# A hybrid decoder layer on eight cores: first tile taken by feature quarters, half of the own activations built during the attention heads, memory copies split over two engines, four output buffers

## What is computed

```python
h = rmsnorm(x, g_pre)
u, v, z_a, c_q, c_kv, k_rope, z_b, q_m, z_m = split(h @ w_in)
y_a = chunked_spatial_gating(u, v, ...) * silu(z_a)      # masked 128x128 per group
y_b = latent_attention(c_q, c_kv, k_rope, ...) * silu(z_b)  # 16 heads, causal
y_m = memory_attention(q_m, mem, ...) * silu(z_m)        # 4 heads into 256 memory tokens
p = einsum('bsnc,ncd->bsnd', stack(y_a, y_b, y_m), w_branch)
merged = sum(sigmoid(h @ w_gate + b_gate) * p, axis=branches)
out = x + rmsnorm(merged @ w_out, g_post)
```

## Time and profile before

| | |
|---|---|
| median of 3 runs | 3443.63 us (3431.74 to 3857.7) |
| the profiled execution | 3429.86 us; its span, first to last instruction of the slowest core, 3428.0 us |
| spans of the cores | 3419.5 to 3428.0 us; mean granted clock 0.981 or 0.982 on all |
| busy | PE 3213.7 us (94%), DVE 1064.1 (31%), ACT 1006.6 (29%), POOL 152.8 (4%) |
| DMA | 208 MB moved; 369.85 MB read from HBM |
| load of one tile, issue to landing | median 16.2 us |
| PE's rate over the tiles | the query latents (line 512) start at 249.05, 293.10 and 336.81 us: 44 us for two tiles |
| the chain that ended last | PE 87%, DVE 5%, DMA 3%, issue 2%, ACT 2% |

### The profile page before, as it was taken

How to read it: one execution, slowest core, us unless ns; L and a number is a source line. 1 busy time by engine, 2 the same in 40 slices (tenths; PEclk the granted TensorE clock), 3 DMA queues, 4 the chain that set the end, 5 groups by cost and what they waited for, 6 DMA issues and landing times.

```text
span 3428.0 us, 62567 instructions; the slowest of 8 cores (3419.5 to 3428.0 us)
## 1 busy us (share of the span) xinstructions
PE 3213.7 (94%) x26432; PEld 1983.9 (58%) x26432; DVE 1064.1 (31%) x1691; ACT 1006.6 (29%) x1192; POOL 152.8 (4%) x289
## 2 busy tenths in 40 slices
PE   2799979999999999999998999889999999999997
PEld 1455557777777777777775544444444444444443
DVE  3444453333333333333334000542524111111115
ACT  1455534444444444444443111011111000000011
POOL 1000000000000000000000111000000000000000
PEclk9899999999999999999999999999999999999998
DMA  8455400000000000000204867344543544445465
GB/s 122 75 99 94 81 4 8 8 8 8 8 8 8 8 8 8 8 8 8 32 14 124 141 111 127 66 80 74 96 80 66 79 75 77 77 74 80 74 135 172
DMA packets 51683, 208.14 MB, mean 61 GB/s; under 512 B 5712, under 2 KB 9936, under 8 KB 47184
## 3 DMA queue, kind: packets, MB, share of 16 engines
q0 software_dynamic: 44496, 174.15, 31.3%
q1 hardware_dynamic: 6912, 29.99, 2.9%
HBM read 369.85 MB, written 8.39 MB: 110 GB/s over the span
## 4 chain that ended last, share of the span: by engine, by line
PE 87%; DVE 5%; DMA 3%; issue 2%; ACT 2%; DVEq 0%; POOL 0%; SPq 0%; ACTq 0%; POOLq 0%
PE ps L312 23%; PE ps L1270 10%; PE ps L790 8%; PE ps L755 7%; PE ps L763 7%; PE ps L731 6%; PE ps L711 6%; PE ps L514 4%; PE ps L1147 3%; PE ps L1317 2%; PE ps L1075 2%; PE ps L758 2%; PE ps L682 1%; PE ps L1052 1%; DMA y<-AR 1%
## 5 line engine op out<-in xcount | busy, mean ns | idle before, releaser
L775 ACT ACTIVATE AR<-ps 128x768 bf16<-128x768 f32 (+1 forms) x656 | 603.6, 920 | 759.5 <-PE ps L763 755.0
L312 PE MATMUL ps<-AR 128*128 128x512 bf16 x3584 | 790.0, 380 | 10.5 <-DVE AR L875 10.5
L312 PEld LDWEIGHTS ps<-AR 128*128 128x128 bf16 x3584 | 350.9, 98 | 430.5 <-issue 14.3
L755 PE MATMUL ps<-AR 128*128 128x256 bf16 (+2 forms) x2176 | 400.5, 279 | 1.1 <-DVE AR L697 1.1
L790 PE MATMUL ps<-AR 128*128 128x129 bf16 x4608 | 372.7, 220 | 1.6 <-ACT AR L775 1.6
L763 PE MATMUL ps<-AR 128*128 128x256 bf16 (+2 forms) x2176 | 358.4, 279 | 0.0
L514 PE MATMUL ps<-AR 128*128 128x512 bf16 x1024 | 274.0, 397 | 76.4 <-DVE AR L422 76.4
L790 PEld LDWEIGHTS ps<-AR 128*128 128x128 bf16 x4608 | 303.2, 98 | 70.3 <-issue 3.3
L1270 PE MATMUL ps<-AR 128*128 128x512 bf16 x1536 | 341.2, 380 | 0.0
L715 DVE CAST AR<-ps 128x512 bf16<-128x512 f32 x256 | 176.9, 691 | 386.5 <-PE ps L711 385.0
L731 PE MATMUL ps<-AR 128*128 128x128 bf16 x4096 | 290.1, 220 | 4.8 <-DVE AR L556 3.7
(11 more groups left out here) (155 smaller groups left out, 2307.9 us busy)
## 6 DMA issues: line engine op xcount, KB each, us to landing
AR<-wts POOLq DMA_DIRECT2D x256, 512.0 KB, 5.8
AR<-xaT POOLq DMA_DIRECT2D x15, 2048.0 KB, 16.2
AR<-xoT SPq DMA_DIRECT2D x16, 512.0 KB, 16.2
AR<-xo SPq DMA_DIRECT2D x8, 1024.0 KB, 8.5
y<-AR SPq DMA_DIRECT2D x8, 1024.0 KB, 11.1
AR<-rows SPq DMA_DIRECT2D x12, 256.0 KB, 6.5
AR<-wcA POOLq DMA_DIRECT2D x4, 576.0 KB, 17.6
AR<-xaT POOLq DMA_DIRECT2D x4, 512.0 KB, 20.1
```

What stands on the lines that cost most here:

```text
L312: ins = h.matmul(ps[:, out_pair_b + half, :], w3[:, k, :], act3[:, k, half * 512:(half + 1) * 512], start=(k == 0), stop=(k == 15))
L755: h.matmul(ps[:, sb + r, i * n:(i + 1) * n], kT[:, kb * 128:(kb + 1) * 128], q_[:, c0:c1], start=(i == 0), stop=False, skip_group_check=True)
L775: sc.add("act", lambda h: h.activation(out=pT[pt][:, :, 0:w], in_=ps[:, sb:sb + 2, 0:w], func=AF.Exp), reads=pregs(sb), writes=(("pT", pt),))
```

## The change

Five edits.

- **Start.** `wcA` and `wcQ` get pages of their own (80 to 97 and 98 to 113 KB), each quarter of `wcA` too. The second tile's load, now in four parts, and then `wcQ` are issued right behind the first tile. The first tile runs by feature quarters: quarter q of all four blocks, then q + 1. DVE scales quarter q one operation of the angles later than before; cosine and sine stand behind the first tile's copies on ACT. The second tile makes its query latent behind its last block instead of its first. The head weights' first load moves from behind tile 0 to behind tile 2.
- **Own activations.** `rstd_o` is inverted in eight pieces in steps 4 to 11 of the first head. Slices 0 to 7 of `hT` lie at 165 to 180 KB and are built in heads 1 to 8, one each: its load at step 0, its scaling at step 26, through two buffers at 137 and 141 KB. Slices 8 to 15 (0 to 15 KB) are loaded and scaled in the last head. The weight ring is 181, 185 and 16 to 28 KB; two pieces of it instead of four are fetched ahead of the last head. The first `proj` waits for `hT` in three parts.
- **Memory attention.** Every second copy of `Ah` goes to ACT. The reciprocal of 1024 columns is cut into four of 256, each with one piece of the next head behind it.
- **Output.** Four buffers each for x and for the result; product and sum by half rows, each half stored as soon as it is done; four loads of x ahead instead of two.
- Addresses of `wo` and `junk` follow.

```diff
-    wc = v3(80, 16, 1088)
+    wca = v3(80, 16, 576)
+    wcq = v3(98, 16, 512)
...
+    load_xa(1, 4)
+    sc.dma("pool", lambda h, sem: h.dma_start(out=wcq[:, :, :], in_=wcQ_d[:, :, :]).then_inc(sem, 16), "wcQ", 1, writes=("wcQ",))
...
+        if u == 0:
+            banks = [rot("mb", 4) for _ in range(4)]
+            for q in range(4):
+                for b in range(4):
+                    lat(b, banks[b], q, 0)
+            for b in range(4):
+                lat_out(b, banks[b])
+            for op in tops[-2:]:
+                op()
+        else:
+            for b in range(4):
...
+                accs = [(b, 0)] + ([(4, 1)] if own and b == (3 if u == 1 else 0) else [])
...
-    sc.add("dve", lambda h: h.reciprocal(out=rstd_o, in_=rstd_o), reads=("rstd_o",), writes=("rstd_o",))
...
+    HT_KB = [165 + 2 * k for k in range(8)] + [2 * k for k in range(8)]
+    STG_KB = [32 + 4 * i for i in range(8)] + [137, 141]
...
-    RING = (165, 169, 173, 177, 181, 185)
+    RING = (181, 185, 16, 20, 24, 28)
...
             if i == n_ab:
+                for k in range(8, 16):
+                    load_stg(k)
+                wsz.prefetch()
                 sc.dma("pool", lambda h, sem: h.dma_start(out=v2(189, 4096), in_=memT[:, :]).then_inc(sem, 16), "memn", 1, writes=("memn",))
-                wsz.prefetch()
-                for k in range(8):
-                    load_stg(k)
-            if i > n_ab and i - n_ab - 1 < 8:
-                scale_stg(i - n_ab - 1)
-                load_stg(i - n_ab + 7)
+            if i >= n_ab + 5 and i - n_ab - 5 < 8:
+                scale_stg(8 + i - n_ab - 5)
+        if hd == 0 and i >= 4 and i < 12:
+            sl = slice((i - 4) * 128, (i - 3) * 128)
+            sc.add("dve", lambda h, sl=sl: h.reciprocal(out=rstd_o[:, sl], in_=rstd_o[:, sl]), reads=("rstd_o",), writes=("rstd_o",))
+        if 1 <= hd < 9:
+            if i == 0:
+                load_stg(hd - 1)
+            if i == n_ab:
+                scale_stg(hd - 1)
...
-    for k in range(8, 16):
-        scale_stg(k)
...
+                if q % 2:
+                    sc.add("act", lambda h: h.activation(out=dst, in_=ps[:, bank, :], func=AF.Copy, scale=MSC), reads=pregs(bank, 1), writes=(("Ah", hm % 2, q),))
...
-        sc.add("dve", lambda h, b=b: h.reciprocal(out=rs, in_=pair(b)), reads=pregs(b), writes=("rs",))
-        for un in nxt[4:8]:
-            un()
+        for q in range(4):
+            sl = slice(q * 256, q * 256 + 256)
+            sc.add("dve", lambda h, b=b, sl=sl: h.reciprocal(out=rs[:, sl], in_=pair(b)[:, sl]), reads=pregs(b), writes=("rs",))
+            for un in nxt[4 + q:5 + q]:
+                un()
...
+        for hf in range(2):
+            hs = slice(hf * 1024, hf * 1024 + 1024)
+            src = obuf[:, j, :] if hf == 0 else pair(b)
...
+            sc.dma("sp", lambda h, sem, j=j, pj=pj, hs=hs: h.dma_start(out=y_d[j * 128:(j + 1) * 128, hs], in_=yo[pj][:, hs]).then_inc(sem, 16),
+                   "yout%d%d" % (pj, hf), 1, reads=(("yo", pj, hf),))
```

More of the change, by code:

```diff
@@ L306, in pregs, with mm32 @@
         return tuple("ps%d" % (b + i) for i in range(n))
-    def mm32(out_pair_b, w3, act3, h):
+    def mm32(out_pair_b, w3, act3, h, ks):
         ins = None
-        for k in range(16):
+        for k in ks:
             for half in range(2):
-                ins = h.matmul(ps[:, out_pair_b + half, :], w3[:, k, :], act3[:, k, half * 512:(half + 1) * 512],
+                ins = h.matmul(ps[:, out_pair_b + half, :], w3[:, k, :], act3(k)[:, half * 512:(half + 1) * 512],
                                start=(k == 0), stop=(k == 15))
@@ L364, in build @@
         place(("kpe2", n), 64 + n, 1)
-    wc = v3(80, 16, 1088)
+    wca = v3(80, 16, 576)
+    wcq = v3(98, 16, 512)
     for q in range(4):
-        sc.place(("wcA", q), *[(80 * 1024 + k * 2176, 1152) for k in range(4 * q, 4 * q + 4)])
-    sc.place("wcQ", *[(80 * 1024 + k * 2176 + 1152, 1024) for k in range(16)])
+        place(("wcA", q), 80 + 4.5 * q, 4.5)
+    place("wcQ", 98, 16)
     xa = [v3(114 + 16 * i, 16, 512) for i in range(2)]
@@ L468, in build @@
                      [("cos", tabs[:, :, 0, :], v16, slice(0, P), KPE), ("sin", tabs[:, :, 1, :], v16, slice(0, P), KPE)])
-    for i, op in enumerate(tops):
+    for i, op in enumerate(tops[:-2]):
         op()
-        if i in (3, 5, 7, 9):
-            q = (i - 3) // 2
-            scale_w(range(4 * q, 4 * q + 4), 0, 576, ("wcA", q))
+        if i in (4, 6, 8, 10):
+            q = (i - 4) // 2
+            scale_w(range(4 * q, 4 * q + 4), wca, ("wcA", q))
     def ang_own(add, a, ra):
@@ L521, in tile_main, with lat, mm @@
-            if b == 1 and u > 0:
-                tile_tail(u - 1)
+            if u > 0:
+                break
+        def lat(b, bank, q, is_q):
+            def mm(h):
+                ins = None
+                for k in range(4 * q, 4 * q + 4):
+                    xs = xt[:, k, b * 128:(b + 1) * 128]
+                    if is_q:
+                        ins = h.matmul(ps[:, bank, :], xs, wcq[:, k, :], start=(k == 0), stop=(k == 15))
+                    else:
+                        h.matmul(ps[:, bank, :], xs, wca[:, k, 0:512], start=(k == 0), stop=(k == 15))
+                        ins = h.matmul(ps[:, kr, b * 64:(b + 1) * 64], xs, wca[:, k, 512:576],
+                                       start=(k == 0 and (u > 0 or b == 0)), stop=(k == 15), skip_group_check=(u == 0))
+                return ins
+            sc.add("pe", mm, reads=(("xa", xb_, q), "wcQ" if is_q else ("wcA", q)), writes=pregs(bank, 1) + (() if is_q else pregs(kr, 1)))
@@ L970, in proj @@
         b = next_pair()
-        sc.add("pe", lambda h: mm32(b, w3, act3, h), reads=(wr,) + tuple(act_regs), writes=pregs(b))
+        for ks in parts:
+            sc.add("pe", lambda h, ks=ks: mm32(b, w3, act3, h, ks), reads=(wr,) + tuple(act_regs[ks.start:ks.stop]), writes=pregs(b))
         return b
@@ L1300, in build @@
     place("gpb", 113, 8)
-    for i in range(2):
-        place(("xob", i), 121 + 8 * i, 8)
-        place(("yo", i), 137 + 52 * i, 8)
-    place("junk", 197, 2)
+    for i in range(NY):
+        place(("xob", i), XO_KB[i], 8)
+        for hf in range(2):
+            place(("yo", i, hf), YO_KB[i] + 4 * hf, 4)
+    place("junk", 161, 2)
     sc.dma("sp", lambda h, sem: h.dma_start(out=gpb, in_=rows_d[0:1, ROW_GPOST:ROW_GPOST + 2048].to_broadcast([P, 2048])).then_inc(sem, 16),
@@ L1322, in build @@
     oss = stat[:, 0:32]
-    load_xob(0)
-    load_xob(1)
+    for j in range(NY):
+        load_xob(j)
     for grp in range(2):
@@ L1363, in build @@
         sems[s] = es.enter_context(nc.semaphore("s%d" % i))
-    final = [("dma:yout0", 64), ("dma:yout1", 64)]
+    final = [("dma:yout%d%d" % (i, hf), 16 * (8 // NY)) for i in range(NY) for hf in range(2)]
     with nc.Block() as block:
```

119 lines of the change are left out of this document (58 added, 61 removed).

## The result

The changed kernel takes 3353.75 us (median; lowest 3342.81), the kernel before 3431.74 us beside it on the same chip: a ratio of 0.9741, 95% interval 0.9707 to 0.9775, so 2.6% faster. Predicted were 3345 us and a range of 3332 to 3370. Two of the five executions of the changed kernel had one or both dies at a much lower clock and took 3880.39 and 3887.55 us; the ratio leaves them out, as it does the one of 3857.7 us of the kernel before.

A forecast was written before the change was run, and what follows sets the result against it. PE was taken as full (87% of the span), gaining only at its few waits and behind its last matmul. Gains 47 + 15.5 + 0.5 + 13 + 11 = 87 from 3429.9 gave 3343, stated as 3345 us, range 3332 to 3370.

The forecast's parts named there:

- Start: First tiles: own pages and earlier loads let the third tile start at 83.4 us instead of 130.3, gain 47.
- Own activations: End of last head: fewer late slices, closing not held up, first projection at the upper clock, gain 15.5 us.
- Heads: Eight heads: one more DVE scaling each costs PE 0 (0 to +9) us; `rstd_o` inverse in pieces gives −0.5.
- Memory: Memory attention: quartered reciprocal removes most of PE's 5.61 us wait; 4.7 us in three heads, −0.3 in the last, gain 13.
- the new wait of 2 us: Memory attention: next scores wait for the second product's copy, 2 us in place of the removed 5.6.
- Output: Output stage: with four buffers DVE needs 5.9 us per block, under PE's 6.9, and follows PE; gain 11 us.
- Shared landing: Start: second tile and `wcQ` share the engines with earlier loads, all landing near 62; 19 us lost, 3364; chance 0.10.
- DVE holding up POOL's transfers: Start: DVE's work on the angles keeps POOL from writing descriptors, `wcQ` 25 us later, 3370; chance 0.04.
- Quicker transfers: Start: longer rows load at 210 GB/s, second tile and `wcQ` down at 54, 8 us sooner, 3337; chance 0.05.

The follow-up runs named there:

- two-buffer kernel: Changed kernel with two output buffers each for results and inputs instead of four, half-row stores kept: output's first matmul to the end 123.2 us, profiled execution 3387.17 us.
- four scalings a head: Changed kernel with each of the eight scalings of own x in heads 1 to 8 done four times: profiled execution 3393.95 us.
- four more edits: Changed kernel plus second tile reordered around `wcQ`, memset of the ones column alone, whole reciprocal, all copies of pieces 4 to 7 by ACT: ratio to before 0.9733.

## Why the prediction was right, and where it was not

**Start (−47, measured −47.5).** Each step came: first matmul at 14, `wcQ` at 61.2, the sums at 79.1, third tile at 82.8. The text was right that the first tile, and with it the order by quarters, "is not what sets the second and third tile". What it didn't say is which edit carries the gain: with the own pages taken away 44.7 us are lost, with the quarters none.

**Own activations (−15.5, measured −17.3).** The number holds, its cause only in part. The prediction gave it to the eight slices moved into the heads and to a slice that lands before the closing. The slices moved are worth 4.0 (7 in the mean over the cores). The step it left out is the division of the first projection, 7.1 us (5 in the mean). With all slices at the end it covers most of DVE's scalings, and the slices moved shorten what it has to cover: two covers over one wait. What the division is worth when the slices are moved was not run.

**Heads (0, and −0.5 for the inverse of `rstd_o`).** PE's waits for the first query copies are 14.2 us, 14.6 before. Right, with a cover of 0.3 us. Ahead of the first head it is −1.1.

**Memory (−13, measured −10.4).** The mechanism was right, the sizes were off by a little each. A quarter of the reciprocal takes 1.76 + 0.1, not 1.69, so four take 7.34 (2194.30 in the last head) and not 6.8, and the periods are 30.2 and not 29.9. The prediction took 34.6 for all three periods of before, by one row; they were 34.62, 34.37 and 34.26. It gave the new wait of 2 us no cost in clock: on core 5 the clock fell behind all three of these waits, and where that reached into the scores (64 matmuls in 14.4 us instead of 13.97) the period was 30.6. The last head, from its scores to the next stage, takes 27.85 us and not 26.6, 1.3 more instead of 0.3. In the two-buffer kernel, whose memory stage is the same and whose scores all kept the upper clock, the stretch was −11.5.

**Output (−11, measured −12.0).** Right in size for core 5, which is where its rows were read; on the other cores, which stores had held up less, the gain is 5 to 10 us. "With four buffers" was not the only way to it: two buffers with half-row stores give nearly all of it too.

**Rivals.** Shared landing: no, `wcQ` came behind the second tile and landed 14.5 us sooner when their places in the queue were changed. DVE holding up POOL's transfers: as a sum of 25 us, no. DVE was busy 16.4 of the 24 us from 12 to 36, and 177 GB/s were moved; 9.8 of 25 us from 36 to 61, 171 GB/s:

```profile
12.00:36.00 24.00, 15.29 (x96) 6.97 (x96) 16.41 (x20) 7.01 (x4) 0.00 (x0) 0.93 1.04 177
36.00:61.00 25.00, 21.34 (x221) 11.88 (x222) 9.79 (x19) 11.90 (x14) 0.53 (x1) 0.93 1.05 171
```

But these rows, and the two of the earlier trace rows, hardly test whether DVE keeps POOL from writing descriptors: POOL has 0 or 1 instructions in each, since it had issued all these loads by 10.4 us here. Where one of its issues and a float32 operation of DVE from SBUF to SBUF do meet, core 5:

```profile
7.92 1.43 POOL L406 DMA_DIRECT2D AR<-xaT  x1
8.00 1.23 DVE L438 TENSOR_SCALAR AR<-AR 128x2048 int32<-128x2048 f32 x1
```

The issue takes 1.43 us, its neighbours 0.55 to 0.64, and it ends at 9.35, 0.12 us behind DVE's operation. It is so in the other kernels as well: when the changed kernel was run again, the issue that met this operation took 1.41 us, and with shared pages two took 1.64 and 1.65. Beside DVE's products with two inputs (5.06 to 7.90) the issues took 0.6. So the rule that the prediction weighed (the Trainium skill, SBUF — State Buffer, "two separate sides") is borne out by this trace, at a price of 0.8 us once; the rival failed because POOL was done before nearly all of DVE's work, and not because the rule doesn't hold. Quicker transfers: no, 171 to 177 GB/s against 165, not 210. These count bytes as they are written, in bf16; x is float32 in HBM, so twice as many are read, about 350 GB/s. The median, 9 us above the forecast, is that of the execution profiled here, in which core 7's lower clock cost 12 us.

## What to carry to other kernels

Ask first which data share a region that is tracked as one: here two weights in one interleaved buffer made loads, scalings and readers wait for each other, and parting them gave over half of the whole gain. Read a stage on all cores before you size it: the output's 12 us were those of the one core that stores held up most. When a change puts two covers over one wait, undo each alone and both together before you credit either. Before giving work to an engine that "has time", measure how long its next consumer can wait: here DVE was idle for two thirds of the time, and yet of 4.2 us more all but 0.3 came out in PE's wait, and the lower clock behind it cost 1.6 to 4 us on top.

## What the hardware showed

PE's clock and its waits: all eight waits of 3.85 us (four scalings a head) were followed by a stretch at the lower clock, of different length. Behind the waits of 2.10 us in the memory heads of the changed kernel the clock fell in all three heads on core 5, and in two of the three on core 4. With four more edits the wait there is 1.47 us, and the clock stays at 1.00 (2096 to 2112 us).

One queue's loads landed in the order of their issue: the second tile's quarters and then `wcQ` at 39.4, 42.0, 45.1, 48.3 and 61.1 us, and with their places changed `wcQ` at 46.6 and then the quarters at 49.9, 52.7, 56.1 and 59.5.

An issue of POOL that meets a float32 operation of DVE from SBUF to SBUF ends about 0.1 us behind it (see the rivals above).

Cores slow down in pairs. In the changed kernel's profile core 7 (and 6 with it) had the first of these windows, core 5 the second (the last three figures are granted clock, DMA share and GB/s):

```profile
160.00:220.00 60.00, 60.00 (x544) 32.86 (x543) 21.22 (x51) 40.71 (x52) 1.05 (x2) 0.81 0.53 83
```

```profile
160.00:220.00 60.00, 58.23 (x655) 34.33 (x654) 21.80 (x55) 40.85 (x55) 1.58 (x3) 0.97 0.50 83
```

The same kernel, run again:

```profile
core 0: 3384.1 us, clock 0.970
core 1: 3382.7 us, clock 0.972
core 2: 3339.9 us, clock 0.986
core 3: 3336.5 us, clock 0.987
...
```

Cores 0 and 1, 2 and 3, 4 and 5, 6 and 7 go together, and another pair was hit hardest, so which pair it is doesn't belong to the kernel. Where it happens does seem to. Core 0 in this execution had a clock of 0.81 over 160 to 220 us and of 0.82 over 2220 to 2340:

```profile
2220.00:2340.00 120.00, 119.99 (x460) 49.55 (x459) 21.47 (x30) 15.39 (x25) 7.92 (x15) 0.82 0.42 71
```

In all profiles of this document the long stretches near 0.81 lie in the same places, the tiles (within 100 to 320 us) and the projections behind the memory attention (within 2200 to 2380 us), and in one kernel behind 3160 us as well. What causes them no run here shows.
